# Even layer: lag matrix moved through device memory, and a new order of products, flips and loads

## Chip, cores and metric

The program runs on one core of one Trainium2 chip, in one launch. The metric is the device time of an execution in microseconds; of several executions the median counts. Engines are named as in the profile: PE (TensorE), ACT (ScalarE), DVE (VectorE), POOL (GpSimd), SP (SyncE, here the engine that issues most DMAs). "Device memory" is the DRAM of the chip; the arena is one large tile in on-chip memory, cut into named views.

## What is computed

A sequence of 256 rows of 1024 features in fp32 goes through two blocks: an even layer (window attention beside a state-space mixer), a feed-forward (FFN) layer, an odd attention layer, another FFN layer, and a second block with an FFN, a mixing layer, attention to a memory of 256 rows and a last FFN. The change touches the even layer alone:

```python
hn = rmsnorm(x, even_norm[i]);  proj = hn @ even_w_in[i]
q, k, v, u = split(proj, [512, 640, 768])
o_attn = swa_sink_attention(rmsnorm(q), rmsnorm(k), v, sinks)     # window of 128, 8 query heads on 2 key heads
# s5_mixer, per group g of 32 (16 channels, 64 complex states):
h_t = lam * h_{t-1} + (w * B) u_t          # lam = exp(a dt), w = (lam - 1) / a
y_t = Re(C h_t) + d * u_t
o_ssm = gelu(y) * sigmoid(gelu(y) @ w_glu + b_glu)
x = x + concat([o_attn, o_ssm]) @ even_w_out
```

## The kernel before

**Weights.** All weight matrices arrive as units of 1 MB (128 partitions x 2048 numbers) in a ring of three raw buffers, loaded by SP in a fixed order (`load`, L557 to L563). From the ninth unit on, ACT makes a rounded high part of each unit (`w_hi`, L1632) and DVE the low part (`w_lo`, L2172), and PE multiplies in passes over both. The first eight units, those of the even layer, are used whole in fp32 (`whole_t`, L712; `whole_n`, L724).

**Order.** Each engine has one program written by hand (`even()` exists once each for PE, ACT, DVE and POOL), and engines wait for each other through semaphores. PSUM is used as two rings of four banks, `acc` and `outp`. A table gives every use of a bank its place in the ring (`ACC` and `OUT`, a plan of names with counts), and a use must wait until the use four places before it is read out (`acc_taken`, `out_taken`; for the reader `emptied`, `out_emptied`). So the order of names in the plan decides which bank a use has and for whom it waits. `flip` (L805) is a transpose on PE against the identity.

**The even layer step by step.** SP loads x, the state-space vectors (L551), the constants, the norm's gain, then B and C (L620, six DMAs; C is loaded as pieces of 64 numbers, twice, so that real and imaginary halves of the state stand side by side in `bc_nat`), and only then the first weight units. PE flips the normed rows, then B and C in one go (64 flips into four `outp` banks), then makes units 0 and 1 (u, L712), flips u by chunks of eight steps, unit 2 (half of q, L724) between them. DVE makes the state tables; PE multiplies chunk states (L1021), does the first half of unit 3, turns the states (L1037) and makes the lag products (L1050): for each group the 16 x 16 response at eight lags. ACT copies them to `lags` (L1840), POOL adds the skip term to lag 0 (L1578). The convolution needs a block-Toeplitz matrix `m_in`: row block j holds the lags shifted by S - 1 - j = 7 - j steps. It is made by 32 DMAs inside on-chip memory, one for each j and each quarter cc of the groups, 18 issued by SP and 14 by ACT:

```python
for j, cc in M_SP:
    sp.dma_start(m_in[PC * j:PC * j + PC, cc, S - 1 - j:, :, :],
                 lags[32 * cc:32 * cc + PC, 0:j + 1, :, :]).then_inc(m_in_done, 16)
sp.wait_ge(m_in_done, 16 * 4 * S)
```

Meanwhile PE does the second half of unit 3, unit 4 (k and v), the swap of the scanned states (L1059) and the flips of q. ACT copies the last projection out (L1811), squares q and k (L1851), DVE sums (L2511), POOL takes roots (L1583, L1584), DVE scales the keys (L2518). PE convolves the first half of the groups (L1086, L1089), flips the keys (waits for L2518), convolves the second half, makes the first window scores (L1121 mask, L1127), flips y, makes the other scores (L1130), then the gated layer (L1161). DVE takes maxima of six score tiles (`front`, L2536 to L2540), halves the gelu output (L2553), normalises (`back`, L2376 to L2378) and forms the gated product (`gated`, L2549), two halves. PE multiplies the gated half with its quarter of the output weights (L1181), flips the probabilities, makes the values (L1197, L1199), and ends with the head half of the output weights (`out_heads`, L694). Between the two calls of `out_heads` stand the flips of the normed memory rows (`norm(8)`), whose result ACT and DVE split into `m_pair` (L1693, L2217). DVE adds the output to x (L2341). The FFN starts with half a unit of memory keys and the flips of the next norm.

## Time and profile before

| | |
|---|---|
| runs | 1214.45 us median of 3 (1213.83 to 1216.28) |
| the profiled execution's own time | 1217.08 us |
| its span | 1215.4 us |
| PE busy | 1187.6 us (98% of the span) |
| DVE / ACT / POOL busy | 782.8 / 588.9 / 64.6 us |
| mean granted PE clock | 0.993 |
| DMA | 206.05 MB, mean 170 GB/s |

Busy time is the sum of an engine's instructions and says little where matmuls overlap; the granted clock is 1.00 at 2.4 GHz and 0.50 at 1.2 GHz. The chain of waits follows back from the last instruction what released what. A record of the timeline gives start and duration of a group of instructions and, in brackets, how long the engine stood idle before it and what ended that. The even layer ends near 142 us; the rest of the program is unchanged.

### The profile page before, as it was taken

The numbers are of one execution on the slowest core, as the hardware profiler recorded it, in microseconds if no ns is written. First come the engines' busy times: TensorE is split into PE (matmuls) and PEld (weight loads), VectorE is DVE, ScalarE is ACT, GpSimd is POOL, SyncE is SP. The second block draws the span as 40 slices with busy tenths as digits, with TensorE's granted clock in tenths as the row PEclk, the third lists the DMA queues.
The fourth block names the chain that finished last, engine by engine and source line by source line (L and its number), as shares of the span: only waits on it lengthen the run. The fifth ranks groups of instructions, "written<-read, shape, count | busy, mean of one in ns | idle before, by whom it ended". The sixth has DMA issues, their size and how long they took to land.

```text
span 1215.4 us, 17637 instructions
## 1 busy us (share of the span) xinstructions
PE 1187.6 (98%) x7043; PEld 1025.4 (84%) x7043; DVE 782.8 (64%) x845; ACT 588.9 (48%) x729; POOL 64.6 (5%) x81
## 2 busy tenths in 40 slices
PE   6989999999999999999999999999999999999997
PEld 5876788888899988888888888888889988888886
DVE  6947666666656457666667666667594646766665
ACT  5437544343566655343435434345574545444443
POOL 2110000000003110000000000000011000000000
PEclk8899999999999999999999999999999999999999
DMA  8243555555554446555555556555533534655551
GB/s 204 91 143 109 187 178 193 187 186 194 173 174 140 139 140 207 176 202 176 199 180 174 190 191 194 186 188 175 191 118 125 177 135 128 202 183 197 180 199 70
DMA packets 158119, 206.05 MB, mean 170 GB/s; under 512 B 9832, under 2 KB 131248, under 8 KB 158064
## 3 DMA queue, kind: packets, MB, share of 16 engines
q1 hardware_dynamic: 157616, 204.51, 51.1%
q10 hardware_dynamic: 448, 0.77, 0.4%
q8 instruction: 39, 0.64, 0.2%
q14 instruction: 16, 0.13, 0.0%
HBM read 203.04 MB, written 1.05 MB: 168 GB/s over the span
## 4 chain that ended last, share of the span: by engine, by line
PE 90%; DVE 5%; ACT 2%; DMA 1%; ACTq 1%; issue 1%; SPq 0%; POOL 0%; POOLq 0%; DVEq 0%
PE outp L754 26%; PE acc L694 20%; PE outp L694 19%; PE outp L757 13%; PE acc L805 3%; PE outp L712 1%; PE outp L724 1%; PE outp L1181 1%; DVE w_lo L2172 1%; DVE h_pair L2217 1%; PE outp L859 1%; DMA raw<-in_even_w_in_dram 1%; ACTq L1847 1%; ACT w_hi L1632 0%; ACT h_pair L1693 0%
## 5 line engine op out<-in xcount | busy, mean ns | idle before, releaser
L1632 ACT ACTIVATE w_hi<-raw 128x2048 fp32r<-128x2048 f32 x177 | 339.5, 1918 | 413.3 <-PE outp L757 285.5
L2172 DVE TENSOR_TENSOR w_lo<-raw,w_hi 128x2048 fp32r<-128x2048 f32 x177 | 405.4, 2290 | 177.5 <-ACT w_hi L1632 177.4
L754 PE MATMUL outp<-h_pair,w_hi 128*128 128x512 f32 x1056 | 266.3, 393 | 0.3
L754 PEld LDWEIGHTS outp<-h_pair,w_hi 128*128 128x128 f32 x1056 | 190.9, 189 | 38.9 <-DVE h_pair L2217 4.2
L757 PEld LDWEIGHTS outp<-h_pair,w_lo 128*128 128x128 f32 x1056 | 144.1, 190 | 10.3
L757 PE MATMUL outp<-h_pair,w_lo 128*128 128x256 f32 x1056 | 147.3, 282 | 0.0
L694 PE MATMUL acc<-w_hi,f_hi 128*128 128x512 f32 x352 | 137.5, 391 | 0.0
L694 PE MATMUL acc<-w_hi,f_lo 128*128 128x512 f32 x352 | 137.3, 390 | 0.0
L694 PE MATMUL acc<-w_lo,f_hi 128*128 128x512 f32 x352 | 137.0, 389 | 0.0
L694 PE MATMUL outp<-w_hi,h_pair 128*128 128x512 f32 (+1 forms) x416 | 114.0, 361 | 0.6 <-DVE w_lo L2172 0.3
L2271 DVE TENSOR_REDUCE arena<-outp 128x256 f32<-128x512 f32 x88 | 56.7, 686 | 59.8 <-PE outp L757 57.5
L2284 DVE TENSOR_REDUCE arena<-outp 128x256 f32<-128x512 f32 x88 | 56.7, 686 | 56.7 <-PE outp L757 56.4
L694 PEld LDWEIGHTS outp<-w_hi,h_pair 128*128 128x128 f32 x416 | 73.0, 189 | 13.8 <-issue 1.6
L754 PE MATMUL outp<-m_pair,w_hi 128*128 128x512 f32 x320 | 80.1, 392 | 0.0
L694 PEld LDWEIGHTS acc<-w_lo,f_hi 128*128 128x128 f32 x352 | 66.1, 188 | 14.1
L694 PEld LDWEIGHTS acc<-w_hi,f_hi 128*128 128x128 f32 x352 | 66.2, 188 | 12.5
L694 PEld LDWEIGHTS acc<-w_hi,f_lo 128*128 128x128 f32 x352 | 66.2, 188 | 12.3
L694 PE MATMUL outp<-w_lo,h_pair 128*128 128x512 f32 (+1 forms) x208 | 74.3, 357 | 0.0
L694 PE MATMUL outp<-h_pair,w_hi 128*128 128x256 f32 x384 | 70.8, 286 | 0.0
L754 PEld LDWEIGHTS outp<-m_pair,w_hi 128*128 128x128 f32 x320 | 57.9, 188 | 11.0 <-issue 0.2
L694 PEld LDWEIGHTS outp<-h_pair,w_hi 128*128 128x128 f32 x384 | 59.9, 191 | 0.9 <-issue 0.5
L1553 POOL TENSOR_SCALAR arena<-arena 128x1 f32<-128x1 f32 x20 | 9.8, 490 | 912.3 <-ACT xn L1655 889.1
(334 smaller groups left out, 1441.2 us busy)
## 6 DMA issues: line engine op xcount, KB each, us to landing
raw<-in_ffn_w_gate_dram SPq DMA_DIRECT2D x44, 1024.0 KB, 5.3
raw<-in_ffn_w_up_dram SPq DMA_DIRECT2D x44, 1024.0 KB, 5.4
raw<-in_ffn_w_down_dram SPq DMA_DIRECT2D x44, 1024.0 KB, 4.8
raw<-in_odd_w_in_dram SPq DMA_DIRECT2D x12, 1024.0 KB, 5.2
raw<-in_w_in_dram SPq DMA_DIRECT2D x10, 1024.0 KB, 5.1
raw<-in_even_w_in_dram SPq DMA_DIRECT2D x5, 1024.0 KB, 9.1
raw<-in_even_w_out_dram SPq DMA_DIRECT2D x4, 1024.0 KB, 5.9
raw<-in_cross_wk_dram SPq DMA_DIRECT2D x4, 1024.0 KB, 5.9
```

The lines of the kernel that those rows point to most:

```text
L694: ins = nc.tensor.matmul(dst, lhs, rhs, start=start and n == 0, stop=stop_ and n == 2, skip_group_check=skip)
L712: ins = nc.tensor.matmul(outp[:, k % NB, m * L:(m + 1) * L], w[:, c, m * P:(m + 1) * P], h_f32[:, c, :], start=c == 0, stop=c == C - 1)
L724: ins = nc.tensor.matmul(outp[:, k % NB, t * UW:(t + 1) * UW], h_f32[:, c, t * P:(t + 1) * P], w[:, c, :], start=c == 0, stop=c == C - 1)
L754: nc.tensor.matmul(bank.rearrange("p (a l) -> p a l", l=L), wh[:, c, :], x[:, :, c, :], start=c == 0, stop=c == C - 1, skip_group_check=True)
L757: ins = nc.tensor.matmul(bank[:, 0:L], wl[:, c, :], x[:, 0, c, :], start=False, stop=c == C - 1, skip_group_check=True)
L805: return nc.tensor.transpose(dst, src, ident[base:base + rows, base:base + rows])
L859: nc.tensor.matmul(outp[:, (k + m) % NB, :].rearrange("p (a l) -> p a l", l=L)[:, :, rows], w[:, c, m * P:(m + 1) * P], m_pair[:, :, c, ro ...
L1181: ins = nc.tensor.matmul(outp[:, (ko + 2 * j + t) % NB, :], sig[:, c, t * P:(t + 1) * P], w[:, c, :], start=c == 0, stop=False, skip_group ...
L1632: A(w_hi[:, slot(u), :], raw[:, u % RAW, :], ACT.Copy).then_inc(w_hi_ready, 1)
L2172: tt(w_lo[:, slot(u), :], raw[:, u % RAW, :], w_hi[:, slot(u), :].bitcast(F32), ALU.subtract).then_inc(w_lo_ready, 1)
L2271: V.reduce_sum(silu[:, j % 2, m * L:(m + 1) * L], bank.rearrange("p (a l) -> p l a", l=L), AX).then_inc(out_free[(k + m) % NB], 1)
L2284: V.reduce_sum(b[:, m * L:(m + 1) * L], bank.rearrange("p (a l) -> p l a", l=L), AX).then_inc(out_free[(k + m) % NB], 1)
```

## The change

- **Lags.** The 32 DMAs go. The four quarters of `lags` are written out to an internal tensor `lag_rows` in device memory (64 rows of 1024 numbers; two DMAs on SP, two on ACT). Both engines wait until all four have landed. Then one DMA per j reads all four quarters back into `m_in`, shifted: j = 7, 5, 3, 1 on SP, 6, 4, 2, 0 on ACT.
- **Loads at the start.** The state-space vectors, B and C are issued by ACT, ahead of all its work, and no longer by SP. C comes in its natural order, once (32 rows of 4 KB each for the real and imaginary part). B and C have semaphores of their own.
- **C's flips.** B's 32 flips stay ahead of unit 0. C's are now 64 matmuls against the identity, one for each of 16 channels, two halves of the state and two parts, written to the upper or lower half of the bank's partitions, and stand between units 0 and 1.
- **Order on PE.** The second half of unit 3 stands ahead of the lag products. The flips of q wait for the first two projection copies only. Both convolutions stand ahead of the keys' flips; then the y flips; then all window scores. `norm(8)` stands ahead of both `out_heads`. The plan of `acc` has y1 ahead of kt.
- **Order on ACT and DVE.** ACT copies unit 3 out ahead of the lag products, and y1, then the gelu table, ahead of the keys. DVE forms the first gated product before it normalises, the second after two score tiles.
- **SP.** Two units of output weights are loaded ahead of the memory rows, which wait for the writes to `lag_rows` only.

```diff
-    OUT = plan([("even_bc", 4), ("even", 5), ("even_sc", 4), ("even_out", 4), ("mem_k1", 1), ("ffn0", 44), ("mem_k0", 1), ("odd", len(ODD_BANKS)),
+    OUT = plan([("even_b", 2), ("even_u0", 1), ("even_c", 2), ("even_u1", 1), ("even", 3), ("even_sc", 4), ("even_out", 4), ("mem_k1", 1), ("ffn0", 44), ("mem_k0", 1), ("odd", len(ODD_BANKS)),
...
-                ("k", 2), ("jg", 2), ("qk", 2), ("y0", 1), ("kt", 1), ("y1", 1), ("yt", 4), ("sc", 2), ("glu", 2),
+                ("k", 2), ("jg", 2), ("qk", 2), ("y0", 1), ("y1", 1), ("kt", 1), ("yt", 4), ("sc", 2), ("glu", 2),
...
+        c_loads = [(bc_nat[G * j + 64:G * j + 64 + G, 0:N * PC], a[n][0].rearrange("g p n -> g (p n)"))
+                   for j, n in enumerate(["ssm_c_re", "ssm_c_im"])]
+        SSM = len(ssm_loads)
+        lag_rows = nc.dram_tensor("lag_rows", (4 * PC, S * 8 * PC), F32, kind="Internal").ap()
+
+        def lags_out(eng, cc):
+
+            eng.dma_start(lag_rows[PC * cc:PC * cc + PC, :],
+                          lags[32 * cc:32 * cc + PC, :, :, :].rearrange("p s i c -> p (s i c)")).then_inc(lag_out, 16)
+
+        def lags_in(eng, j):
+
+            eng.dma_start(m_in[PC * j:PC * j + PC, :, S - 1 - j:, :, :].rearrange("p a s i c -> p a (s i c)"),
+                          lag_rows.rearrange("(a p) m -> p a m", p=PC)[:, :, 0:(j + 1) * 8 * PC]).then_inc(m_in_done, 16)
...
-                for j, cc in M_SP:
-                    sp.dma_start(m_in[PC * j:PC * j + PC, cc, S - 1 - j:, :, :],
-                                 lags[32 * cc:32 * cc + PC, 0:j + 1, :, :]).then_inc(m_in_done, 16)
-                sp.wait_ge(m_in_done, 16 * 4 * S)
+                for cc in range(2):
+                    lags_out(sp, cc)
+                sp.wait_ge(lag_out, 16 * 4)
+                for j in (7, 5, 3, 1):
+                    lags_in(sp, j)
+                for j in range(2):
+                    load(u0 + 6 + j, quarter(w_out, 1, j), 512)
                 sp.dma_start(mem_sb, a["mem_2"][0].rearrange("(t p) f -> p t f", p=P)).then_inc(mem_in, 16)
-                for kh in (1, 0):
-                    for j in range(2):
-                        load(u0 + 8 - 2 * kh + j, quarter(w_out, kh, j), 512)
+                for j in range(2):
+                    load(u0 + 8 + j, quarter(w_out, 0, j), 512)
...
+                pe.wait_ge(b_in, 16 * 2)
                 for p in range(PC):
-                    for j in range(4):
-                        rows = bc_nat[G * j:G * j + G, :]
-                        ins = flip(outp[:, (OUT["even_bc"] + j) % NB, p * G:(p + 1) * G],
-                                   rows[:, p::PC] if j < 2 else rows[:, p * P:(p + 1) * P], G, G * j)
+                    for j in range(2):
+                        ins = flip(outp[:, (OUT["even_b"] + j) % NB, p * G:(p + 1) * G],
+                                   bc_nat[G * j:G * j + G, p::PC], G, G * j)
                 ins.then_inc(bc_flipped, 1)
-                whole_t(u0, k0, fresh=chunks(0))
-                whole_t(u0 + 1, k0 + 1)
+                whole_t(u0, OUT["even_u0"], fresh=chunks(0))
+                pe.wait_ge(c_in, 16 * 2)
+                for j in range(2):
+                    out_taken(pe, OUT["even_c"] + j)
+                for p in range(PC):
+                    for h in range(2):
+                        for j in range(2):
+                            rows = slice(G * (j + 2), G * (j + 3))
+                            ins = nc.tensor.matmul(outp[N * h:N * h + N, (OUT["even_c"] + j) % NB, p * G:(p + 1) * G],
+                                                   bc_nat[rows, p * N:(p + 1) * N], ident[rows, rows],
+                                                   start=True, stop=True)
+                ins.then_inc(bc_flipped, 1)
+                whole_t(u0 + 1, OUT["even_u1"])
...
+                whole_n(u0 + 3, k0 + 3, (1,))
...
-                out_emptied(pe, k0 + 2, 3)
+                out_emptied(pe, k0 + 2, 2)
...
                 convolve(0)
-                k = ACC["kt"]
-                acc_taken(pe, k)
-                pe.wait_ge(qk_ready, 1)
-                for t in range(T):
-                    ins = flip(acc[:, k % NB, t * P:(t + 1) * P], qkv[:, t, 512:640])
-                ins.then_inc(acc_ready, 1)
                 convolve(1)
...
+                k = ACC["kt"]
+                acc_taken(pe, k)
+                pe.wait_ge(qk_ready, 1)
+                for t in range(T):
+                    ins = flip(acc[:, k % NB, t * P:(t + 1) * P], qkv[:, t, 512:640])
+                ins.then_inc(acc_ready, 1)
...
+                emptied(pe, ACC["qk"], 2)
+                emptied(pe, ACC["kt"])
+                pe.wait_ge(mask_ready, 1)
+                window_scores(0)
                 window_scores(1)
                 window_scores(2)
...
+                norm(8)
                 out_heads(0, True)
-                norm(8)
                 out_heads(1)
...
+                for dst, src in ssm_loads:
+                    nc.scalar.dma_start(dst, src).then_inc(ssm_in, 16)
+                for dst, src in b_loads:
+                    nc.scalar.dma_start(dst, src).then_inc(b_in, 16)
+                for dst, src in c_loads:
+                    nc.scalar.dma_start(dst, src).then_inc(c_in, 16)
...
+                qkv_out(1)
                 for j in range(2):
                     k = ACC["k"] + j
                     written(act, k)
                     A(lags.rearrange("p s i c -> p i s c")[:, 4 * j:4 * j + 4],
                       acc[:, k % NB, :].rearrange("p (i s c) -> p i s c", i=4, c=PC),
                       ACT.Copy).then_inc(acc_free[k % NB], 1)
-                qkv_out(1)
                 act.wait_ge(kz_ready, 1)
                 act.wait_ge(k_ready, 1)
-                for j, cc in M_ACT:
-                    nc.scalar.dma_start(m_in[PC * j:PC * j + PC, cc, S - 1 - j:, :, :],
-                                        lags[32 * cc:32 * cc + PC, 0:j + 1, :, :]).then_inc(m_in_done, 16)
+                for cc in (2, 3):
+                    lags_out(nc.scalar, cc)
+                act.wait_ge(lag_out, 16 * 4)
+                for j in (6, 4, 2, 0):
+                    lags_in(nc.scalar, j)
...
                 y_out(0)
-                qk_out(ACC["kt"], k_t, L, 1)
                 y_out(1)
                 nc.scalar.preload_act_table_set("gelu_apprx_tanh_and_others")
+                qk_out(ACC["kt"], k_t, L, 1)
...
+                gated(0)
                 back(0)
                 back(1)
-                gated(0)
-                back(2)
                 gated(1)
-                for nth in range(3, 6):
+                for nth in range(2, 6):
                     back(nth)
```

Three places of the order, as each engine's program has it. First PE at the start, before (L805 flips; `outp<-arena` are B and C, L712 units 0 and 1, `acc<-arena` the flips of u):

```order
L805 MATMUL acc<-arena 128x32 x2
L805 MATMUL acc<-arena,xn 128x128 x16
L805 MATMUL outp<-arena 128x32 x64
L712 MATMUL outp<-h_whole,raw 128x256 x32
L805 MATMUL acc<-arena 32x128 x16
```

and now (L812 the flips, L719 units 0 and 1, L988 C's products with the identity):

```order
L812 MATMUL acc<-arena 128x32 x2
L812 MATMUL acc<-arena,xn 128x128 x16
L812 MATMUL outp<-arena 128x32 x32
L719 MATMUL outp<-h_whole,raw 128x256 x16
L988 MATMUL outp<-arena 64x32 x64
L719 MATMUL outp<-h_whole,raw 128x256 x16
```

C's 32 flips left the stretch ahead of unit 0 and came back as 64 products between the units.

Second PE from the second half of the convolution to the first scores, with its waits, before (L805 128x128 the keys, 128x32 y; L1121 and L1127 the scores):

```order
L805 MATMUL acc<-arena 128x128 [waits qk_ready,acc_free0]
L805 MATMUL acc<-arena 128x128
L1086 MATMUL acc<-arena_end,arena 32x128 [waits acc_free1]
...
L1121 MATMUL outp<-h_pair 128x512 [waits mask_ready,acc_free0,out_free1,acc_free2,acc_free1]
L1121 MATMUL outp<-h_pair 128x512 [waits out_free2]
L1127 MATMUL outp<-arena 128x128 x8
L805 MATMUL acc<-arena 128x32 [waits acc_free2,acc_free1,acc_free3]
L805 MATMUL acc<-arena 128x32 [waits acc_free3]
L805 MATMUL acc<-arena 128x32 [waits acc_free0]
L805 MATMUL acc<-arena 128x32 [waits acc_free1]
```

and now (bank 0 is y1's and bank 1 the keys'):

```order
L812 MATMUL acc<-arena 128x128 [waits qk_ready,acc_free1]
L812 MATMUL acc<-arena 128x128
L812 MATMUL acc<-arena 128x32 [waits acc_free2,acc_free0,acc_free3]
L812 MATMUL acc<-arena 128x32 [waits acc_free3]
L812 MATMUL acc<-arena 128x32 [waits acc_free0]
L812 MATMUL acc<-arena 128x32 [waits acc_free1]
L812 MATMUL acc<-arena 128x32 x28
L1132 MATMUL outp<-h_pair 128x512 [waits mask_ready,acc_free1,out_free1,acc_free2]
L1132 MATMUL outp<-h_pair 128x512 [waits out_free2]
L1138 MATMUL outp<-arena 128x128 x8
```

The y flips stand ahead of the scores, and their fourth wait, for bank 1, is now for the copy of the keys.

Third ACT from the lag copies on (L1840 and now L1863), before:

```order
L1840 ACTIVATE arena<-acc 128x4x8x16 [waits acc_ready] x2
L1808 ACTIVATE arena<-outp 128x4x64 [waits w_used]
L1808 ACTIVATE arena<-outp 128x4x64
L1847 DMA arena_end<-arena 16x640 [waits k_ready,kz_ready]
L1847 DMA arena_end<-arena 16x640
L1847 DMA arena_end<-arena 16x768 x4
L1847 DMA arena_end<-arena 16x896 x4
L1847 DMA arena_end<-arena 16x1024 x4
L1811 ACTIVATE arena<-outp 128x2x256 [waits w_used]
```

and now:

```order
L1863 ACTIVATE arena<-acc 128x4x8x16 [waits acc_ready] x2
L516 DMA lag_rows<-arena 16x1024 [waits k_ready,kz_ready]
L516 DMA lag_rows<-arena 16x1024
L521 DMA arena_end<-lag_rows 16x4x896 [waits lag_out]
L521 DMA arena_end<-lag_rows 16x4x640
L521 DMA arena_end<-lag_rows 16x4x384
L521 DMA arena_end<-lag_rows 16x4x128
L1833 ACTIVATE arena<-outp 128x2x256 [waits w_used]
```

Fourteen DMAs became six, with a wait for `lag_out` between the second and the third, ahead of the last projection copy.

## Rows read from the trace of the kernel before

**Rows 1.** The page, part 2 (40 slices of 30.4 us; granted clock in tenths)
```profile
PEclk8899999999999999999999999999999999999999
```

**Rows 2.** The chain of waits, start of the program (start us, us, what)
```profile
7.38 9.13 DMA raw<-in_even_w_in_dram
```

**Rows 3.** Waits of PE, 60 to 148 us (us in total, times, longest)
```profile
PE acc L805 <- DVE arena L2518: 1.8, 1, 1.8
...
PE acc L805 <- ACT arena L1811: 1.4, 1, 1.4
...
PE outp L694 <- DVE w_lo L2172: 1.4, 1, 1.4
...
PE outp L1181 <- DVE arena L2549: 1.0, 1, 1.0
```

**Rows 4.** Timeline, all engines, 0 to 30 us (start us, us, engine ...)
```profile
0.79 0.44 SPq L548 DMA_DIRECT2D x_sb<-in_x_dram  x1
...
0.80 1.28 ACT L1655 ACT_TABLE_LOAD   x1 [0.80 <-PEq L2815]
...
6.04 1.29 SPq L620 DMA_DIRECT2D arena<-in_ssm_c_im_dram  x2
...
6.27 0.61 ACT L1655 ACTIVATE xn<-x_sb 128x512 f32<-128x512 f32 x1
...
7.38 6.12 SPq L563 DMA_DIRECT2D raw<-in_even_w_in_dram  x3
...
8.22 0.86 POOL L1553 TENSOR_SCALAR arena<-arena 128x1 f32<-128x1 f32 x1
...
8.97 3.87 PE L805 MATMUL acc<-arena,xn 128*128 128x128 f32 x16 [0.60 <-DVE xn L2206]
...
13.82 1.95 PE L805 MATMUL outp<-arena 32*128 32x32 f32 x64 [0.98 <-DMA arena<-in_ssm_c_im_dram]
...
17.01 13.22 PE L712 MATMUL outp<-h_whole,raw 128*128 128x256 f32 x46 [1.24 <-DMA raw<-in_even_w_in_dram]
...
18.69 2.05 ACT L1788 ACTIVATE arena<-outp,arena 128x512 f32<-128x512 f32 x2
```

**Rows 5.** DMA issues (engine, op, count, KB each, median us to landing)
```profile
x_sb<-in_x_dram SPq DMA_DIRECT2D x1, 1024.0 KB, 4.8
...
arena<-in_ssm_c_im_dram SPq DMA_DIRECT2D x2, 128.0 KB, 6.8
...
arena_end<-arena ACTq DMA_DIRECT2D x4, 64.0 KB, 2.3
...
out_dram<-xn SPq DMA_DIRECT2D x2, 512.0 KB, 2.7
```

**Rows 6.** Timeline, all engines, 60 to 92 us
```profile
61.97 1.97 PE L1037 MATMUL acc<-arena 128*64 128x128 f32 x32
...
67.56 11.38 SPq L632 DMA_DIRECT2D arena_end<-arena  x18
...
74.53 3.62 PE L724 MATMUL outp<-raw,h_whole 128*128 128x256 f32 x16
...
79.59 1.07 PE L805 MATMUL acc<-arena 128*128 128x128 f32 x8 [1.44 <-ACT arena L1811]
...
87.42 1.16 PE L1127 MATMUL outp<-arena 64*128 64x128 f32 x16
...
88.52 0.69 PE L805 MATMUL acc<-arena 32*128 32x32 f32 x32
```

**Rows 7.** Stretches of time, PE (us, PE busy (x), clock, DMA share, GB/s)
```profile
16.00:17.00 1.00, 0.00 (x0) 0.69 1.09 345
...
22.00:23.00 1.00, 1.00 (x4) 0.50 0.57 69
...
23.00:24.00 1.00, 1.00 (x5) 0.90 0.17 53
```

**Rows 8.** Timeline, DVE, 91 to 148 us
```profile
120.78 0.69 DVE L2382 TENSOR_TENSOR h_pair<-acc,h_pair 128x512 fp32r<-128x512 f32 x1 [0.61 <-ACT h_pair L1958]
```

More of the change, by code:

```diff
@@ L548, in _ @@
             sp.dma_start(x_sb[:, :, :], a["x"][0].rearrange("(t p) f -> p t f", p=P)).then_inc(x_loaded, 16)
-            if "even" in running:
-                for dst, src in ssm_loads:
-                    sp.dma_start(dst, src).then_inc(ssm_in, 16)
             sp.dma_start(early, a["consts"][:, 0:EARLY_W]).then_inc(consts_in, 16)
@@ L618, in _ @@
                 w = by_p(a["even_w_in"][0])
-                for dst, src in bc_loads:
-                    sp.dma_start(dst, src).then_inc(bc_in, 16)
                 for j, n in enumerate([3, 4, 0]):
@@ L957, in even @@
             def even():
-                u0, k0 = UNITS["even"], OUT["even"]
+                u0, k0 = UNITS["even"], OUT["even"] - 2
                 pe.wait_ge(consts_in, 16)
@@ L1072, in even @@
                     ins.then_inc(acc_ready, 1)
-                pe.wait_ge(m_in_done, 16 * 4 * S)
+                pe.wait_ge(m_in_done, 16 * S)
                 pe.wait_ge(h_ready, 1)
@@ L1763, in even @@
             def even():
-                u0, k0 = UNITS["even"], OUT["even"]
+                u0, k0 = UNITS["even"], OUT["even"] - 2
+                for dst, src in ssm_loads:
[4 more added lines that the diff above has]
+                    nc.scalar.dma_start(dst, src).then_inc(c_in, 16)
                 act.wait_ge(x_loaded, 16)
@@ L1784, in even @@
                 A(small[:, 15, :], turns[:, 1, :], ACT.Sin, scale=TWO_PI).then_inc(lam_sin, 1)
-                act.wait_ge(bc_flipped, 1)
-                for j, part in ((2, cr), (3, ci)):
-                    k = OUT["even_bc"] + j
+                act.wait_ge(bc_flipped, 2)
+                for j, part in ((0, cr), (1, ci)):
+                    k = OUT["even_c"] + j
                     A(part.rearrange("p g c -> p c g"), outp[:, k % NB, :].rearrange("p (c g) -> p c g", g=G),
@@ L2398, in even @@
             def even():
-                u0, k0 = UNITS["even"], OUT["even"]
+                u0, k0 = UNITS["even"], OUT["even"] - 2
                 dve.wait_ge(x_loaded, 16)
```

30 lines of the change are left out of this document (10 added, 20 removed).

## Prediction

> **What bounds the kernel now.** I read the page first [rows 1]: TensorE (PE) is busy nearly all of the span, so time can be won only where PE stands still, runs at the lower clock, or does needless work. The clock row says where to look: only the first two slices (0 to 61 us, the even layer) are below 9 tenths. Then the chain of waits [rows 2]: up to 16.50 it is the load of the first weight unit, which SP issues only at 7.38 behind nine smaller DMAs, then PE. Then the waits of PE from 60 to 148 us [rows 3]: 1.8 us for the scaled keys, 1.4 for the last projection copy (behind ACT's 14 DMA issues), 1.0 for the gated product, 1.4 for the low part of the memory unit's weights. Everything the change touches lies before 148 us; behind it PE runs without such gaps, so a shift there reaches the end whole. The sum is made on the profiled execution: its own time 1217.08 us, span 1215.4, so 1.68 us lie around the span. It stands 2.63 us above the median of the runs, 1214.45.
>
> **The start, up to unit 1.** Before: x is issued at 0.79 and lands 4.8 us later [rows 4, 5]; the norm's flips run from 8.97 to 12.84; the 64 B and C flips wait for the last C load until 13.82 and end at 15.77; unit 0 starts at 17.01 when its weights land [rows 4]. Now:
> - SP issues x, two small loads and unit 0. By its 0.47 us rhythm unit 0 is issued at 2.2 instead of 7.38. Before its last byte come x, constants, B, C and itself, about 3.0 MB; x shows 1 MB in 4.8 us with about 2.3 of it fixed [rows 5], so some 2.5 us per MB: landed by about 11. It is no longer last.
> - ACT issues seven DMAs ahead of its table load. At 0.63 us each (SP's 18 lag issues took 11.38 [rows 6]) it is through at 5.2, with the 1.28 us table at 6.5, where x is now used at about 6.1 (I allow 0.5 us because B's packets share the last of x's transfer). ACT's two squares (0.6 us each) then end at 7.8. GpSimd needs them only for its second row, at 8.22 + 0.5 = 8.7 [rows 4]. So 0.9 us of cover: at nothing, but if it is gone, each microsecond counts.
> - The norm's flips end at 13.35, half the 64 flips (B's 32) take 0.98, and unit 0 starts at 14.45: **-2.55 us** (bounds -3.1 with x undelayed, 0 with the weights late).
> - Clock: the granted clock falls within the 16 to 17 us row to 0.50 (1.2 GHz) and is back at 2.4 GHz by about 23.1 [rows 7], after PE had done only short flips and waited. The first 6.1 us of unit 0 run at half speed, which costs 3.05 us. Unit 0 now starts at the high level. If the clock falls at 16.3 all the same and comes back as long after the unit's start as before (14.45 + 6.1), 4.25 us are low and cost 2.1: 0.9 won. If it doesn't fall, 3.05. The middle: **-2.0**.
> - C flips: 32 transposes become 64 matmuls against the identity, because C is now loaded in natural order and each half state is turned apart. An fp32 matmul shows as two records (a half unit's 8 matmuls are 16 [rows 6]), a transpose as one, so 64 are 128. The nearest small rows: 1.95 us for 64 transposes (30.5 ns) [rows 4], 1.16 us for 16 fp32 records of 128 columns on two row groups (72 ns), 1.97 us for 32 records with 64-column weights on all rows (62 ns), 0.69 us for 32 (21.6 ns) [rows 6]. C's weights have 64 columns on two row groups, half of the second: 128 x 30.5 = 3.9 us (bounds 2.8 and 7.9). The transposes' 0.98 us are already counted out of the start, so **+3.9** on the path, between unit 0 and unit 1.
> - ACT copies C out (2.05 us [rows 4]) only after these, between unit 0 and unit 1, with its copy of unit 0 behind it; both are done within unit 1, which takes twice a half unit's 3.6 us, and the sines behind them feed nothing before 64 us. DVE gets B's flips sooner and C's 10 us before it uses them. All this at nothing; the cover is unit 1's 7.2 us.
>
> Up to the start of unit 1: -2.55 - 2.0 + 3.9 = **-0.65 us** (27.2 before: bounds -4.7, with 2.8 and the whole clock, and +6).
>
> **Lags.** Times here are on before's axis, the start's shift left aside. A half unit of the projection (8 matmuls, 3.62 us) now runs ahead of the lag products, so the first lag DMA, 67.56 before, is issued 3.65 us later, at 71.2 [rows 6]. Then: two issues per queue (1.2 us), 64 KB each out. The nearest rows are 2.3 us for 64 KB inside the chip and 2.7 for 512 KB to device memory [rows 5]: out by 74.2. Four issues per queue back, 1.18 MB together: by x's 4.8 us for 1 MB, 5.0 here: landed at **79.2** (before: 18 DMAs on SP issued until 78.94). PE: the qk flips no longer wait for the last projection copy, so the 1.44 us gap goes and they end at 80.66 - 1.44 = 79.2 [rows 6]. Both arrive together: convolutions at 79.4 instead of 80.73, **-1.3**. Behind the waiting queues: on SP two weight loads and the memory rows, needed after 99; on ACT the last projection copy, which PE allows only at 78.15 (74.53 + 3.62), when ACT is free at 76.7.
>
> The Trainium skill (DMA: Bandwidth & Descriptors, Anatomy of one DMA) speaks against the detour: a completion waits for the write's receipt, and that can be surprisingly long when the target is device memory. The store row (2.7 us, data included) does not show that, so it stays a rival.
>
> **Convolutions to the end of the layer.** The keys' flips move behind both convolutions: these end at 83.3, the keys are scaled at 83.9 by the same chain as before (its head, the last projection copy, no longer waits for ACT's issues, -0.5). Of the 1.8 us wait [rows 3] 0.6 is left. But ACT now copies y1, loads the gelu table (1.28 [rows 4]) and only then copies the keys: 85.8. And the fourth y flip needs the keys' bank, which was y1's before (the order of PE that stands with the change has the wait). So the y flips, cheap at 0.69 [rows 6], end at 86.55 and the first scores start at 86.6 against 86.75: only -0.15 of the 1.3 is left. From there the y flips are out from between the scores; the gated layer starts with the maxima, -0.35. Then DVE does its gated product before the two backs: the 1.0 us wait of [rows 3] goes but for 0.1: **-1.25** at the output products. The memory norm's flips go ahead of the head products: their last bank is freed by the second low part (ends at 121.47 [rows 8]; the values leave PE at about 120.1), so PE idles about 1.2 us more; but w_lo of the next unit is then ready: its 1.4 us wait goes, and 0.3 us at the next norm's flips: another -1.25. At the FFN: **-2.5**.
>
> **Sum:** -0.65 - 2.5 = -3.15 us: 1217.08 - 3.15 = 1213.9 for this execution, 1214.45 - 3.15 = **1211.3 us** for the median.
>
> **Rivals.**
> 1. *ACT's issues hold up the norm (ends slower).* SP's weight issues took 6.12 us for three [rows 4], 2.04 each, with the rings full. If ACT's four B and C issues take that too, ACT is free at 0.8 + 3 x 0.63 + 4 x 2.04 = 10.9, its squares end at 13.5 against the 8.7 that GpSimd can bear; unit 0 starts at 19.2 and the clock's 2.0 us are lost too: -3.15 + 4.8 + 2.0 = +3.65, **1218.1**. It makes the kernel slower once the squares end some 1.2 us beyond 8.7. Against: SP's two issues of C's imaginary part took 1.29 us [rows 4], ahead of the weights. Chance 0.13.
> 2. *C flips at 62 ns a record*: 7.9 us, +4.0: **1215.3**. For it: the two passes of one fp32 matmul use the same row group. Against: the 72 ns row has twice the columns. The skill (TensorE: Matmul & The Clock Gate, Part 2) says loads run ahead only if the row groups do not conflict; by that the pair of passes would serialise. No row shows this shape. Chance 0.14.
> 3. *The round trip is late*: if the last return, issued at 76.1, takes the 6.8 us of C's loads [rows 5], it lands at 82.9 and the convolutions start at 83.1 instead of 79.4, +3.7: **1215.0**. For it: source and target are rows of 0.5 to 4 KB, and the detour is two trips in series. Against: C came in pieces of 256 bytes while the rings were full. Chance 0.15.
> 4. *The clock never falls* before the C flips (-1.05), whose records take 21.6 ns (-1.1): **1209.1**. Chance 0.13.
> 5. The forecast, 1209.8 to 1212.8 by itself: 0.45.
>
> **Numbers.** A measurement of this kernel tells 0.2% (2.4 us) from no change: the three runs spread over 2.45. Faster: 0.35 of the forecast, rival 4's 0.13, so 0.48. Same: 0.10 of the forecast, most of 2 and 3 (0.23): 0.33. Slower: rival 1's 0.13 and the rest of 2 and 3 (0.06): 0.19. The range 1208.3 to 1216.0 leaves out rival 1 and the tails of 2 to 4.
>
> **What would show it.** Unit 0's first matmul at 14 to 15 us; 128 records between units 0 and 1 in about 4 us; clock row between 16 and 23 us; convolutions at 79.4 less the start's shift, waiting on neither queue by more than 0.5 us; a table load between y1's and the keys' copy with PE waiting for the latter; no wait before L1197; a wait of about 1.2 us inside the memory norm's flips. Wrong if unit 0 starts after 16, or the lags come back over 1 us after the qk flips.

## The result and the profile after

| | before | after |
|---|---|---|
| median of 16 runs each | 1214.57 us (1213.83 to 1216.87) | 1221.88 us (1216.80 to 1224.03) |
| after to before | | 1.0054, 95% interval 1.0046 to 1.0061 |
| profiled execution, own time | 1217.08 us | 1218.92 us |
| its span, mean granted clock | 1215.4 us, 0.993 | 1217.2 us, 0.994 |

The change makes the kernel slower by 7.3 us; 1211.3 was forecast, and the range ended at 1216.0. The two profiled executions are only 1.8 us apart, since before's is one of its slowest and after's one of its fastest. A second profile of the changed kernel (run change_again) was therefore taken at 1224.03 us, two more of the kernel before (before_again, before_third) at 1214.95 and 1214.48.

The start, TensorE, on the timeline (start us, us, engine line op, shapes, count, idle before and releaser); it answers to [rows 4]:

```profile
13.22 1.97 PE L812 MATMUL outp<-arena 32*128 32x32 f32 x32
...
15.35 8.59 PE L719 MATMUL outp<-h_whole,raw 128*128 128x256 f32 x32 [0.15 <-DMA raw<-in_even_w_in_dram]
23.87 2.07 PE L988 MATMUL outp<-arena 32*64 32x32 f32 x128
25.87 7.17 PE L719 MATMUL outp<-h_whole,raw 128*128 128x256 f32 x32
```

Unit 0 starts at 15.35 instead of 17.01; the 128 records of the C products take 2.07 us; unit 1 starts at 25.87. B's 32 flips take 1.97 us: as long as the 64 of before. Behind them unit 0 waits once more for its weights (0.15 us). The chain of waits, against [rows 2], gives their transfer (start us, us, what):

```profile
2.27 13.04 DMA raw<-in_even_w_in_dram
```

It is issued 5.1 us earlier than before and lands only 1.2 us earlier, at 15.31.

The waits of TensorE from 0 to 150 us (us in total, times, longest), against [rows 3]:

```profile
PE acc L1103 <- DMA arena_end<-lag_rows: 5.1, 1, 5.1
PE acc L812 <- ACT arena L1880: 1.5, 1, 1.5
...
PE acc L812 <- DVE h_pair L2406: 0.6, 1, 0.6
```

Gone are 1.8 (keys), 1.4 (projection copy), 1.0 (gated product) and 1.4 (w_lo). In their place stands one wait of 5.1 us for the lags' read-back. SP's queue and the landings, against [rows 6] and [rows 5]:

```profile
70.00 0.80 SPq L516 DMA_DIRECT2D lag_rows<-arena  x2
73.70 1.73 SPq L521 DMA_DIRECT2D arena_end<-lag_rows  x4
```

```profile
arena_end<-lag_rows SPq DMA_DIRECT2D x1, 256.0 KB, 4.7
...
arena_end<-lag_rows SPq DMA_DIRECT2D x1, 192.0 KB, 6.7
...
arena_end<-lag_rows ACTq DMA_DIRECT2D x1, 32.0 KB, 8.2
```

Out in 3.7 us, back in 9.5: landed at 83.23. Before, the last on-chip move was issued at 78.9 and the convolutions ran at 80.73. What the pause does, in both profiles of the changed kernel (stretch, length, TensorE busy and instructions, granted clock, DMA share, GB/s), first the one at 1218.92, then the one at 1224.03:

```profile
83.00:86.00 3.00, 2.72 (x52) 0.52 1.05 388
93.00:100.00 7.00, 6.65 (x44) 1.00 0.00 0
```

```profile
83.00:86.00 3.00, 1.50 (x29) 0.56 1.05 319
86.00:90.00 4.00, 4.00 (x83) 0.50 1.06 395
93.00:100.00 7.00, 6.48 (x55) 0.54 0.00 0
```

The granted clock falls to its lower level (1.2 GHz) towards the end of the pause. In the quicker execution it is back at 2.4 GHz by 86.5. In the other it stays low until 90, and falls again after the next pause (0.4 and 1.5 us ahead of y's flips, 91 to 93.5).

### The profile page after: what moved, and what is told of

Its sections match the earlier page's. It is cut to its first block, busy times and chain, and to the rows that moved or that the text cites. A ratio compares the mean times of both kernels' runs of the same rounds, so it can differ in the third digit from the quotient of the medians.

```text
span 1217.2 us, 17807 instructions
## 1 busy us (share of the span) xinstructions
PE 1189.2 (98%) x7139; PEld 1027.9 (84%) x7139; DVE 782.9 (64%) x845; ACT 589.1 (48%) x729; POOL 67.9 (6%) x81
## 4 chain that ended last, share of the span: by engine, by line
PE 92%; DVE 3%; DMA 2%; ACT 2%; issue 0%; ACTq 0%; SPq 0%; POOL 0%; POOLq 0%
PE outp L761 26%; PE outp L701 20%; PE acc L701 20%; PE outp L764 13%; PE acc L812 3%; PE outp L719 1%; PE outp L731 1%; PE outp L1197 1%; DMA raw<-in_even_w_in_dram 1%; DVE w_lo L2196 1%; DVE h_pair L2241 1%; PE outp L866 1%; DMA arena_end<-lag_rows 1%; PE acc L1177 1%; ACT w_hi L1648 0%; ACT h_pair L1709 0%
```

## The experiments

### The four parts

**Each part alone, on the kernel before.** trip_alone puts in `lags_out`/`lags_in` and takes out the 32 moves (SP also waits for the read-back before its next loads). start_alone has the start's part of the diff. half_alone has this:

```
+                whole_n(u0 + 3, k0 + 3, (1,))
                 pe.wait_ge(bb_ready, 2)
...
-                whole_n(u0 + 3, k0 + 3, (1,))
```

(and ScalarE's `qkv_out(1)` ahead of its copies of the lags).

> The kernel before with the round trip alone: lags out to device memory in 4 transfers and back in 8, start and orders as before. If the trip costs what the change's trace shows: lags ready at 71.5, landed out at 74.7, back at 82.5 to 84, the convolutions 1.5 to 3.5 us later than the 80.73 of before, and the kernel 1 to 6 us slower than before (1216 to 1220). If it is as fast as I forecast (back at 79.2): 1213 to 1214, 0 to 1.5 under before.

> The kernel before with the new start alone (ScalarE issues the early loads, C in natural order and as matmuls behind unit 0): unit 1 starts 1.3 us earlier (25.9 instead of 27.2) with C's 128 records at 16 ns each. If this reaches the convolutions and the end: 1212 to 1213.5 us. If the moves and their DMA hide it: 1214 to 1215. If the granted clock of the first 60 us comes out lower in most runs: 1216 or more, with a mean clock at or under 0.992 in the runs.

> The kernel before with unit 3's second half ahead of the lag products, and nothing else of the change. If the half unit is what loses the time: k_ready and the first transfer of the lags 2.7 us later (about 70.2 instead of 67.5), the last landed at 83.5, TensorE waits 2.5 to 3.5 us more ahead of the convolutions (with the keys' flips and scores behind them), and 3 to 8 us slower than before (1218 to 1223). If it only costs together with the trip or the new order of the flips: within 1.5 us of before (1214 to 1216).

**One part undone in the changed kernel.** direct_moves has before's 32 moves and load order back. half_back has the half unit behind the lag products. flips_back has the keys' flips between the convolutions again, scores(0) ahead of y's flips, and ScalarE's keys' copy ahead of y1's.

> The changed kernel with its round trip alone undone: 32 on-chip transfers of the lags and the load order of before; the new start and the new order of the convolutions, flips and norm(8) stay. Theory (the round trip lost the time): the moves land about 80.5 us, the convolutions start there instead of at 83.3 (before: 80.73, less up to 1.3 from the start), the waits behind shrink, and the time is 1211 to 1215 us, 7 to 10 under the change. Rival (the new order of the flips and of norm(8) lost it): 1218 us or more, and the convolutions again start by 80.5. Second rival (the start's cost, a clock that runs low in the first 60 us in most runs): 1217 or more, with a mean clock at or under 0.992.

> The changed kernel with unit 3's second half put back behind the lag products (and ScalarE's copy of it behind the lags'), the start, the trip and the other orders kept. The half unit held k_ready back by its 2.6 us. If the wait for the lags is what costs: the read-back lands at about 80.7 instead of 83.3, the wait of 5.1 shrinks to about 2.5, and the time is 2.5 to 5 us under the change (1217 to 1219.5), the upper part of that if the shorter pause spares the clock. If the order of the keys' flips costs alone: within 1 us of the change (1221 to 1223).

> The changed kernel with the keys' flips between the two convolutions again, the first window scores ahead of y's flips and ScalarE's order of before; start, trip, half unit and norm(8) as in the change. The wait for the lags stays at 5 us. If the second pause (0.4 and 1.5 us at 89 to 91) and the low clock behind it cost: 2 to 5 us under the change (1217 to 1220). If only the wait for the lags matters: within 1 us of the change.

| run | median us | to before, 95% interval |
|---|---|---|
| trip_alone | 1216.01 | 0.9999 to 1.0020 |
| start_alone | 1217.15 | 1.0008 to 1.0026 |
| half_alone | 1217.64 | 1.0011 to 1.0030 |
| the whole change | 1221.88 | 1.0046 to 1.0061 |
| direct_moves | 1222.95 | 1.0049 to 1.0075 |
| half_back | 1215.68 | 0.9996 to 1.0022 |
| flips_back | 1218.55 | 1.0014 to 1.0033 |

My first theory falls with direct_moves: without the round trip the changed kernel is no faster (1222.95), and its convolutions start later still. Waits and SP's queue of direct_moves:

```profile
PE acc L1103 <- DMA arena_end<-arena: 5.7, 1, 5.7
```

```profile
70.19 12.37 SPq L639 DMA_DIRECT2D arena_end<-arena  x18
84.02 0.38 SPq L642 DMA_DIRECT2D arena<-in_mem_dram  x1
```

From the first issue to the last landing the moves take 13.8 us here and the trip 13.2 in the changed kernel. In trip_alone it is 14.6 us (65.31 to 79.89) with a pause of 2.4 us, and the time is 1.1 us over before's, with an interval that reaches down to no difference. (The lags land earlier than the 82.5 to 84 expected because the profile reaches them earlier, with v's flips at full clock.) The trip wins nothing and loses little. start_alone, over 1216, has the time of the third of its cases but not its sign: its eleven executions have mean clocks of 0.995 to 0.998, not 0.992 or less. It is taken up below. The half unit is what costs most: taking it back is worth 6.2 us of the 7.3, more than the 2.5 to 5 that I expected. Of the lags nothing can start before `k_ready`, so 3.6 us of useful work ahead of the lag products push the whole 13 us chain back by nearly that, while TensorE does not reach the wait any later. half_back's waits, its convolutions and its clock:

```profile
PE acc L1103 <- DMA arena_end<-lag_rows: 2.6, 1, 2.6
```

```profile
80.98 0.43 PE L1103 MATMUL acc<-arena_end,arena 128*32 128x128 f32 x8 [2.56 <-DMA arena_end<-lag_rows]
```

In this profile the pause is 2.6 us instead of 5.1, the clock stays, and each group of eight takes 0.4 us instead of 0.65. Its other executions spread from 1213.76 to 1222.01, so this need not hold in each. half_alone shows the same loss from the other side (first issue 70.83 instead of 67.56, convolutions at 83.85 instead of 80.73), if smaller than expected: 2.8 us; its profile has no wait for the keys any more, 1.8 us in [rows 3].

Put in alone, the three parts cost 1.1, 2.2 and 2.8 us, together 6.1 of the 7.3. Taken out alone, the trip, the half unit and the order of the flips give -1.1, 6.2 and 3.3 us, together more than 7.3: what a part costs depends on the others. The order of the flips was not run by itself; what is left for it beside the three is 1.2 us. That it costs more in the change because it puts a second pause behind the first fits the profiles (scores at full clock in flips_back, at the lower level in change_again below), but flips_back also takes a pause of 1.5 us out, and no run separates the two.

### Is it the clock?

filled puts flips whose result nobody reads into the pause:

```
+                for i in range(36):
+                    flip(acc[:, k % NB, i % 4 * P:(i % 4 + 1) * P], qkv[:, i % 2, 0:P])
                 pe.wait_ge(m_in_done, 16 * S)
```

> The changed kernel with 36 needless 128x128 flips on TensorE (36 x 130 ns = 4.7 us) between the flips of q and k and the wait for the lags; nothing else is moved, the lags land when they landed. If the pause as such is all: 0 to 1 us slower than the change. If the clock that falls after the pause is the reason why most runs of the change are 3 to 5 us over its profiled one: the groups of 8 take 0.41 us and not 0.65 from the first, scores and all behind run at full clock, and the time is 1216 to 1218.5.

> The changed kernel itself, for a second profile. Its profiled run (1218.92) was among its fastest; the median is 3 us over it. If the clock makes the difference: a run at 1221 to 1224 shows the lower level longer than the first one's 3.4 us behind the wait for the lags, and again behind the second pause at 89 to 92, as two of its variants do. If it is the transfers: the lags land 2 us or more later than 83.2, at the same clock.

filled: 1219.41 us (1.0024 to 1.0055), 2.5 us under the change, though it only adds work. That points to the clock, but weakly: its interval overlaps the change's (1.0046 to 1.0061), its six runs go from 1214.62 to 1223.51, and it landed above the 1218.5 I expected. The profiled one is the fastest, with the clock at 1.00 throughout and the convolutions' groups at 0.43; of its lead of 4.2 us at the first scores, 2.7 are there before the convolutions start, from a quick unit 0 (7.17 us) and quick v's flips (5.79), and 1.5 come behind the pause. change_again is the better evidence, since the two profiles of the one kernel are within 0.2 us of each other up to the pause: 1224.03 us, the lags landed at about 84.5, 1.2 us later than in the first profile, while scores start 2.7 us and the gated layer 5.0 us later. So of the 5.1 us between the two, 1.2 are the transfers, 1.5 the lower level in the convolutions and 2.3 the lower level in the scores. Its timeline:

```profile
84.50 0.65 PE L1103 MATMUL acc<-arena_end,arena 128*32 128x128 f32 x8 [6.19 <-DMA arena_end<-lag_rows]
...
94.46 1.22 PE L1132 MATMUL outp<-h_pair 128*128 128x512 f32 x2
95.61 2.08 PE L1138 MATMUL outp<-arena 64*128 64x128 f32 x16
...
102.37 7.20 PE L1177 MATMUL acc<-arena,raw 128*128 128x256 f32 x32
```

The same 16 score products take 1.16 us in [rows 6].

How long the pause must be is less clear than these two profiles suggest. I add up TensorE's idle time between the last projection unit and the first product with the lags in all 20 profiles. The ten with 3.2 us or more all run some of those products at the lower level. The four with 1.5 us or less do not. Of the six with 2.0 to 2.6 us two do (start_alone, and before_again, a profile of the kernel before, with groups of 0.66 us from 78.91) and four do not (before_third, start_again, filled, half_back).

### Why is the read-back slow?

loads_behind lets SP wait for `m_in_done` ahead of its output weights and memory rows. read_wide and read_x change `lags_in` alone, for its timing:

```
-            eng.dma_start(m_in[PC * j:PC * j + PC, :, S - 1 - j:, :, :]...
+            eng.dma_start(m_in[64 * (j % 2):64 * (j % 2) + 64, ...   (read_wide)
-                          lag_rows.rearrange("(a p) m -> p a m", p=PC)...
+            src = a["mem_2" if j % 2 else "x"][0][64 * (j // 2):64 * (j // 2) + 64, :]   (read_x)
```

> The changed kernel, except that the two output weight units and the memory load are issued only when the lags are back. If their 1 MB behind the read-back is what made it land at 83.2: it lands by 80.5, the convolutions start there, 3 to 4 us under the change. If the read-back is slow by itself (its descriptors go to 16 partitions each, or all of them read one small region): it lands at 82.5 to 83.5 and the time stays within 1 us of the change, or 1 to 3 more because the output weights come later than out_glu wants them.

> The changed kernel, but each of the 8 transfers of the read-back writes its 64 pieces to 64 partitions instead of 16 (same source, same pieces of 512 to 4096 bytes, same bytes and count; the lags come to lie in the wrong places, so what is computed from them is not the reference's). If the read-back goes at 150 GB/s because each transfer writes only 16 partitions: it lands 3 to 4.5 us after its issue (77.5 instead of 83.2). If its source is what makes it slow: again 8 us. Only the landing is read here.

> The changed kernel, but the 8 transfers of the read-back take their 64 pieces each from rows of the inputs x and mem_2, 64 other rows for each transfer, instead of all from the one small tensor just written (same destinations, sizes and count; so the lags are replaced by input values). If the shared, just written source makes the read-back slow: it lands 3 to 4.5 us after its issue. If the 16 partitions per transfer do, or the size of the pieces: again 8 us. Only the landing is read here.

loads_behind: 1220.83 us (1.0026 to 1.0060), and the last return still takes 8.4 us with no other load behind it: not the competition. read_x: 7.9 to 8.9 us from other sources: not the just written tensor. read_wide, last return of each queue:

```profile
arena_end<-lag_rows SPq DMA_DIRECT2D x1, 64.0 KB, 5.2
arena_end<-lag_rows ACTq DMA_DIRECT2D x1, 32.0 KB, 5.4
```

5.4 instead of 8.2 us with the same pieces and source, spread over 64 partitions instead of 16. So the narrow target is a part of it. But the issues take longer here (2.7 instead of 1.8 us), and from the first issue to the last landing it is 7.5 us (73.72 to 81.18) instead of 9.5: 2.1 of the 4.5 us over my forecast. 3 to 4.5 us to the landing were expected, and what is left above that was not separated. The DMA engines are counted as full all along, at less than half the rate (stretches of after; the last three figures are clock, DMA share, GB/s):

```profile
75.00:82.00 7.00, 1.00 1.07 164
83.00:90.00 7.00, 0.76 1.05 395
```

### The start

> The kernel with the new start alone, with 14 needless 128x128 flips (14 x 130 ns = 1.8 us) in TensorE's pause ahead of the flips of q and k (2.2 us there, 1.4 in the kernel before). If the start alone is slower than before because TensorE comes earlier to a wait that is no shorter, so that the longer pause lets the clock fall (0.50 from 80.3 to 83.4 in its profile): the clock stays, the convolutions' groups take 0.41 us, and the time is 1214 to 1215.5, 1.5 to 3 under start_alone. If its 2.2 us come from elsewhere: again 1216.5 to 1217.5.

> The kernel before itself, for a second profile. Its profiled run (1217.08, clock 0.993) was among its slowest; most runs stand at 1214 to 1215 with a clock of 0.997 to 0.999. If I took time out of the start that most runs do not lose: a run at 0.997 or more shows the full clock in the first unit (17 to 23 us) or in v's flips (47 to 54 us) or in both, and the 2.0 us that the forecast booked for the clock are not there to be won. If the low clock at 17 to 23 us is in this profile too: the booking was right and the loss is elsewhere.

> The same once more, since one profile is one execution: what is common to both, and what goes with the run's time, in the clock at 17 to 23 and at 47 to 54 us.

> The kernel with the new start alone, for a second profile. If the time of its typical run (1217.15, over before by 2.2) is the clock: v's flips at 46 to 54 us or the convolutions at 80 to 84 us run at the lower level here, where those of before do not. If both kernels look alike there: the 2.2 us are elsewhere, and stay open.

start_filled (14 flips of the identity in the pause ahead of the flips of q and k): 1216.63 us (1.0003 to 1.0021), 0.5 under start_alone, within the noise; the pause explains at most a part. Its clock stays behind the pause, as intended, and the time is the same. The other three profiles explain more. First before_again, then before_third (stretches of TensorE; clock, DMA share, GB/s):

```profile
17.00:21.00 4.00, 3.97 (x10) 1.00 1.10 349
44.00:50.00 6.00, 5.57 (x64) 1.00 0.39 147
```

```profile
17.00:20.00 3.00, 3.00 (x7) 0.51 1.10 349
```

The 0.50 that I took for the rule from 16.3 to 23.1 [rows 7] is absent from the clock row in before_again and over by 19.5 in before_third. The row is not the whole story: before_again's line counts 10 records in 4 us, the pace of the lower level, and only from 21 on are there 6 or 7 in each. Units 0 and 1 take 17.11 us in the profile that I read, 15.90 and 15.52 in these, against 8.59 + 7.17 = 15.76 after. v's flips, which take 9.0 us at the lower level, take 5.79 in before_again and 7.46 in before_third. They begin at 45.62, 44.43 and 44.01 in the three profiles of before, at 45.20 and 45.91 in the two of the start alone:

```profile
45.91 7.46 PE L812 MATMUL acc<-arena 32*128 32x32 f32 x64 [1.10 <-ACT arena L1823]
```

So the start wins against the one profile that I had read, and is about 1.3 us later than the other two. All 20 profiles say the same of what lies ahead: the flips of u, behind units 0 and 1, begin at 33.2 us on average with the old start (6 profiles, 32.3 to 34.0) and at 33.7 with the new one (14 profiles, 31.7 to 35.5). Behind it the lags' issues are no faster: SP's 18 take 11.50 us, ScalarE's 13 behind the first 9.15 instead of 8.40 (start_alone). Whether that, the clock or chance makes up the rest of the 2.2 us stays open.

### Mended

early_states moves the 64 products of the carried states, which need no lags, ahead of the wait. As written there (`start=True` in every group) it leaves out a part of the carried states' share of the sums; the instructions and their order are those of the intended kernel.

```
+                convolve(0, 0)
+                convolve(1, 0)
                 pe.wait_ge(m_in_done, 16 * S)
+                convolve(0, 1)
+                convolve(1, 1)
```

> The changed kernel with the convolutions' other half (the carried states times w_out_c, 32 matmuls per bank that need no lags) ahead of the wait for the lags: 16 groups of 8, some 3.4 us of useful work into the pause of 5.1 us. The work behind the wait is halved: if the wait is the bound, glu starts 3.4 us earlier plus what the clock gives back, 3 to 7 us under the change (1215 to 1219). If another chain (the rms of the keys, y's copies on ScalarE) stands right behind: only 0 to 1.5 us.

> The changed kernel with what the runs showed put right: the half unit behind the lag products again, the carried states' half of both convolutions (64 matmuls, 2.0 us) ahead of the wait for the lags with only the first product of each bank's rows starting the sum, the keys' copy ahead of the table load, norm(8) behind the first output heads again. The lags land at about 81.0, the convolutions are over at 83.0 instead of 84.7, and no pause is over 1.5 us, so the clock stays. If so: 1.5 to 3 us under half_back, 1212 to 1214, under both kernels. If the keys' rms (82.9) and the softmax chain on VectorE come last anyway: 1214 to 1216, the same as before.

> The start of the kernel before with everything behind it as in mended: trip through device memory, half unit behind the lag products, the carried states' half of the convolutions ahead of the wait for the lags, keys' copy ahead of the table load, the new softmax order on VectorE, norm(8) behind the first heads. If the new start loses (its C products add 2.1 us on the path, and unit 0, started 1.6 us earlier, is over no earlier than in the second and third profile of the kernel before): 0.5 to 2 us under mended, 1211.5 to 1213. If the start is neutral: 1213 to 1214. If it wins in this company: over 1214.

early_states: 1218.99 us (1.0021 to 1.0042), 2.9 under the change, a little less than expected: 2.04 us of work (not 3.4) moved into a pause that stays 3.5 us long, and the clock still falls. In mended, `start=i == 0` for the states' products and the lags' products only add; the sums are whole. Its waits from 60 us on and the products:

```profile
PE outp L701 <- DVE w_lo L2199: 1.4, 1, 1.4
...
PE acc L812 <- DVE arena L2545: 0.5, 1, 0.5
PE acc L1105 <- DMA arena_end<-lag_rows: 0.5, 1, 0.5
PE acc L812 <- ACT arena L1883: 0.4, 1, 0.4
```

```profile
77.98 2.04 PE L1102 MATMUL acc<-arena 128*32 128x128 f32 x64
80.51 1.96 PE L1105 MATMUL acc<-arena_end,arena 128*32 128x128 f32 x64 [0.49 <-DMA arena_end<-lag_rows]
...
84.57 0.73 PE L1135 MATMUL outp<-h_pair 128*128 128x512 f32 x2
```

**mended: 1213.42 us, 0.9976 to 0.9994 of before**: 1.4 us under the kernel before, 8.5 under the change. Scores start at 84.57 (91.74 after). With the old start (mended_old_start) 1213.84 us, 0.9983 to 1.0001: the start is neutral in this company, the second of the three cases.

Mended undoes several things at once, and one of them, by the rows, should have stayed. With norm(8) behind the first heads again, the 1.4 us wait for w_lo is back. The issue of the FFN's up weights, the change first, then mended:

```profile
143.10 0.54 SPq L570 DMA_DIRECT2D raw<-in_ffn_w_up_dram  x1
```

```profile
137.86 0.54 SPq L570 DMA_DIRECT2D raw<-in_ffn_w_up_dram  x1
```

The first output products start at 104.38 and 97.20, so this stretch takes 38.7 us in the change and 40.7 in mended, as it does in before (100.75 to 141.50); half_back, flips_back and filled, with the change's order of norm(8), all have 38.7. Behind it the change needs some 0.3 us more to the end. So that order would take another 1.6 us or so off mended; that is an estimate from these rows, and no run shows it.

## Why the prediction was wrong

The forecast was 3.15 us faster; the medians are 7.3 us apart the other way. In the two profiles first read, the difference builds up like this (us, the change less before):

| stretch | forecast | measured |
|---|---|---|
| up to the end of unit 1 (flips of u at 33.95 and 32.88) | -0.65 | -1.07 |
| from there to the convolutions (80.73 and 83.28) | -1.3 | +3.62 |
| to the first scores (86.75 and 91.74) | +1.15 | +2.44 |
| to the issue of the FFN's up weights (141.50 and 143.10) | -2.35 | -3.39 |
| together | -3.15 | +1.60 |

The other 5.5 us between the medians lie in which executions were profiled: before's is 2.5 us over its median, the change's 3.0 under.

**Start, -2.55: -1.66.** x, ACT's seven issues, the table and the squares came as forecast (x used at 6.10, squares over by 7.57, GpSimd's second row at 8.67; rival 1 did not happen). Two steps failed. "Half the 64 flips (B's 32) take 0.98": they took 1.97. Before, the flips went round four row groups, now round two, and each takes 62 ns instead of 30. And "landed by about 11. It is no longer last": the weights landed at 15.31 and were still last, by 0.15 us, so quicker flips would have won no more than that. By after's DMA rows 3.6 MB had moved by then, 250 GB/s on average; the forecast had 3.0 MB at 400.

**Clock, -2.0: about -1.4 in this profile, next to nothing against the other two.** The clock row stays at 1.00, as rival 4 has it, and yet unit 0 takes 8.59 us where unit 1 takes 7.17. The error is the method: the sum was made on one execution and shifted to the median as it stood, but a low clock that lasts this long in one execution of three cannot be saved in the others.

**C flips, +3.9: +2.07** (16 ns a record; the lower bound was 2.8, and rival 2's 62 ns, its price for two passes in series, did not come). In sum the start wins 1.07 us, where 0.65 was forecast: errors in opposite directions that nearly cancel, which is luck.

**The round trip, -1.3: +3.62.** The failed step, and the largest, is "by x's 4.8 us for 1 MB, 5.0 here": 8.2 us from issue to landing, 9.5 from the first issue. The first issue came as forecast (71.2 less the start's 1.07; 70.00 measured), and the way out took 3.7 us instead of 3.0. x fills 128 partitions; each transfer here fills 16, which accounts for 2.1 us of the 4.5 that are over. Rival 3 had the place (lags landed at 82.9, convolutions at 83.1; 83.23 and 83.28 measured), at a chance of 0.15. That its times fit so well is partly luck: they stand on before's axis, where the convolutions come at 84.35. Its price of 3.7 us left out what stands next.

**What was missing altogether: the pause's effect on the clock.** Rival 3 priced TensorE's idle time at its length. It costs 1.5 us more in the convolutions of one profile and 2.7 in the other (5.3 and 6.5 us against 3.8 in filled), and 2.3 more in the scores where the level falls again behind the next pause. The change's executions spread over 7 us where before's spread over 3, and the mean clock goes with them, from 0.996 (1216.80) to 0.991 (1224.03); but half_back spreads over 8 us with a pause half as long, so the pause is not shown to be the cause of the spread. The same profile had shown me the mechanism at 16 to 23 us, and I used it there, only for a gain.

**The half unit ahead was booked only as a shift of 3.65 us in the lags' issue**, which the quicker trip was to absorb. Had I costed this move alone with before's 13 us of moves, it would have come out at about +3; with the trip measured as slow as the moves, that is what it is.

**Behind the convolutions** the forecast held, the clock left aside. The keys' copy behind the table makes y's flips wait 1.5 us; the waits of 1.0 for the gated product and 1.4 for w_lo are gone, norm(8)'s flips wait 0.6 (1.2 forecast). From the first scores at +5.0 us against [rows 6] the kernel comes down to +1.6 at the FFN: SP's load of the FFN's up weights is issued at 143.10 instead of 141.50. That is 3.4 us regained, somewhat more than the forecast's 2.35; 2.0 of it lie behind the output products, where norm(8) moved and 1.25 were forecast.

The Trainium skill (DMA: Bandwidth & Descriptors, Anatomy of one DMA) warns of the completion receipt when the target is device memory. The traces show little of it: the four stores of 64 KB landed 2.0 to 3.3 us after their issue, the on-chip moves of 64 KB after 2.3 [rows 5]. No run separates the receipt from the rest, and it is not where the time went.

## What to carry to other kernels

- Work moved ahead of the instruction that starts a long chain of transfers lengthens the pause at its other end by its whole length. Work that needs no result of the chain (here half of the convolutions' products) belongs behind the issue and ahead of the wait.
- Cost a pause of TensorE at its length plus the low clock behind it, and look at a second profile before booking any saving of clock. Take the price of a transfer from a row with as many target partitions, not as many bytes.
- When a change of several parts is slower, take the parts out one by one and read each one's own stretch before undoing it: norm(8)'s new place won 2 us inside a change that lost 7.

## What the runs showed of the hardware

- A read-back of 1.18 MB into 16 partitions per transfer runs at about 150 GB/s with the DMA engines counted as fully busy; into 64 partitions the last return lands in 5.4 instead of 8.2 us, and the whole is 2.1 us shorter.
- 64 flips of 32 rows going round four row groups: 1.95 us; 32 going round two: 1.97 us. Yet 128 records of fp32 products with 64-column weights, also round two, take 2.07 us, 16 ns each. They alternate between the upper and the lower half of the output partitions as well; whether that is what makes them quick was not tried.
- Unit 0 takes 7.17 us in filled and read_x, 8.59 in after and 9.81 in mended, with the clock row at 1.00 in all four; in mended TensorE does 3 or 4 records per us until 21, as it does at 0.50 elsewhere. The granted clock as profiled does not tell the pace of these first microseconds. Why is open.
- v's flips take 5.8, 7.5 or 9.0 us from run to run, in kernels old and new, with the clock low for none, some or all of them.
